# Stick-breaking stages of a head pair two weight units apart, and the S5 input stage of layer 1 one unit later

## The reference, cut to what matters

```python
z = jnp.einsum('bhqd,bhkd->bhqk', qb, k).astype(jnp.float32) * scale
log_1mb = jnp.where(mask, jax.nn.log_sigmoid(-z), 0.0)
later = lax.cumsum(log_1mb, axis=3, reverse=True) - log_1mb
w = jnp.where(mask, jnp.exp(jax.nn.log_sigmoid(z) + later), 0.0)
return jnp.einsum('bhqk,bhkd->bhqd', w.astype(v.dtype), v)
```

## The kernel before, in words

| pause of unit | layer 0 before | layer 1 before | layer 0 and 1 after |
|---|---|---|---|
| 6 | sb_s 0 (and mm_k in layer 0) | sb_s 0 | the same |
| 7 | sb_u 0 | sb_u 0 | none |
| 8 | sb_p 0, sb_s 1 | the same | sb_u 0, sb_s 1 |
| 9 | sb_u 1 | the same | none |
| 10 | sb_p 1, sb_s 2 | the same | sb_p 0, sb_u 1, sb_s 2 |
| 11 | sb_u 2 | the same | none |
| 12 | sb_p 2, sb_s 3 | and ssm_in 0 | sb_p 1, sb_u 2, sb_s 3 |
| 13 | sb_u 3, ssm_in 0 | sb_u 3, ssm_in 1 | ssm_in 0 |
| 14 | sb_p 3, ssm_in 1 | sb_p 3, ssm_in 2, ssm_out 0 | sb_p 2, sb_u 3, ssm_in 1 |
| 15 | ssm_in 2, ssm_out 0, turn | ssm_in 3, ssm_out 1, turn | ssm_in 2, ssm_out 0, turn |
| 16 | da_s 0, ssm_in 3, ssm_out 1 | da_s 0, ssm_out 2 | sb_p 3, da_s 0, ssm_in 3, ssm_out 1 |
| 17 | da_t 0, da_s 1, ssm_out 2 | da_t 0, da_s 1, ssm_out 3 | da_t 0, da_s 1, ssm_out 2 |
| 18 | da_p 0, da_t 1, da_s 2, ssm_out 3 | da_p 0, da_t 1, da_s 2 | with ssm_out 3 |

## Time and profile before

### The profile page before, as it was taken

One profiled execution on the slowest core, in us unless ns is written; L12 is line 12 of the kernel. 1 busy time (PEld: TensorE's weight loads), 2 busy tenths in 40 slices (PEclk: granted clock), 3 DMA queues, 4 the chain that ended last, 5 costly groups with the idle time before them and its releaser, 6 DMA issues. The chain is left out here.

```text
span 1025.0 us, 17644 instructions
## 1 busy us (share of the span) xinstructions
PE 990.7 (97%) x6784; PEld 877.4 (86%) x6784; DVE 765.7 (75%) x1185; ACT 550.5 (54%) x843; POOL 46.2 (5%) x104
## 2 busy tenths in 40 slices
PE   6999999999999999999999999999999999999996
PEld 6977899999897888888889779999988878888885
DVE  5988997888765866889765569787887567666665
ACT  7455436475755645544464663545656565444543
POOL 5004000000000004000000110000000000000000
PEclk9999999999999999999999999999999999999999
DMA  8797438556644666686657853465665446666661
GB/s 330 240 187 181 124 104 268 147 169 182 182 145 123 247 187 185 195 222 190 195 145 203 178 149 100 142 197 149 180 181 167 141 127 188 191 193 189 185 190 78
DMA packets 64163, 181.37 MB, mean 177 GB/s; under 512 B 19728, under 2 KB 21776, under 8 KB 63440
## 3 DMA queue, kind: packets, MB, share of 16 engines
q1 hardware_dynamic: 63648, 179.91, 60.6%
q10 hardware_dynamic: 432, 0.32, 0.1%
HBM read 176.67 MB, written 3.54 MB: 176 GB/s over the span
## 5 line engine op out<-in xcount | busy, mean ns | idle before, releaser
L1288 DVE TENSOR_TENSOR s_w_lo<-s_raw,s_w_hi 128x1024 fp32r<-128x1024 f32 x312 | 374.9, 1228 | 95.4 <-ACT s_w_hi L914 91.6
L914 ACT ACTIVATE s_w_hi<-s_raw 128x1024 fp32r<-128x1024 f32 x312 | 320.8, 1054 | 183.1 <-PE p_T L1876 76.7
L1874 PE MATMUL p_T<-s_hT,s_w_hi 128*128 128x256 f32 x576 | 165.8, 288 | 0.7 <-ACT s_w_hi L914 0.7
L1875 PE MATMUL p_T<-s_hT,s_w_hi 128*128 128x256 f32 x576 | 162.9, 283 | 0.0
L1876 PE MATMUL p_T<-s_hT,s_w_lo 128*128 128x256 f32 x576 | 162.8, 283 | 0.0
L1874 PE MATMUL p_A<-s_w_hi,s_bT_hi 128*128 128x512 f32 x320 | 125.1, 391 | 2.5 <-DVE s_bT_lo L1288 2.5
L1876 PE MATMUL p_A<-s_w_hi,s_bT_lo 128*128 128x512 f32 x320 | 124.7, 390 | 0.0
L1875 PE MATMUL p_A<-s_w_lo,s_bT_hi 128*128 128x512 f32 x320 | 124.6, 389 | 0.0
L1874 PEld LDWEIGHTS p_T<-s_hT,s_w_hi 128*128 128x128 f32 x576 | 110.2, 191 | 4.6 <-issue 2.7
L1875 PEld LDWEIGHTS p_T<-s_hT,s_w_hi 128*128 128x128 f32 x576 | 110.3, 192 | 0.1
L1876 PEld LDWEIGHTS p_T<-s_hT,s_w_lo 128*128 128x128 f32 x576 | 110.3, 192 | 0.0
(11 more groups left out here) (269 smaller groups left out, 1844.1 us busy)
## 6 DMA issues: line engine op xcount, KB each, us to landing
s_raw<-in_weights SPq DMA_DIRECT2D x312, 512.0 KB, 3.7
s_bt<-in_ssm_bt SPq DMA_DIRECT2D x2, 1024.0 KB, 7.3
s_gates<-f_turn SPq DMA_DIRECT2D x16, 128.0 KB, 7.5
s_x<-in_x SPq DMA_DIRECT2D x1, 1024.0 KB, 10.0
s_dv<-in_ssm_bc SPq DMA_DIRECT2D x2, 512.0 KB, 8.6
u_turn<-s_st_y SPq DMA_DIRECT2D x4, 256.0 KB, 4.7
s_uB<-u_turn SPq DMA_DIRECT2D x16, 64.0 KB, 5.1
s_bt<-in_mem SPq DMA_DIRECT2D x1, 1024.0 KB, 7.0
```

The costliest lines, as they stand in the source:

```text
L914: return nc.scalar.activation(o, i, f, **kw)
L1288: return V.tensor_tensor(o, i0, i1, op)
L1874: mm(o, lhi, rhi, start=first, stop=False, **kw)
L1875: mm(o, lhi, rlo, start=False, stop=False, **kw)
```

## The change

The sums stage moves from one unit after the scores to two, the value products from two units after to four. The banks of sb_u are A0 and A1 in place of X0 and X1. The four ssm_in take A2, X0, A1, A1 in place of A0, A1, A0, A1. `FIRST` of layer 1 becomes 13, so all ssm stages and GELU of layer 1 come one unit later, and with them the two places in SyncE's order where the result of the S5 branch is written out and read back (`turn_y`, from chunk positions 45 and 48 to 47 and 50).

```diff
-FIRST = [13, 12]
+FIRST = [13, 13]
...
     for p in range(SB_PAIRS):
         after(6 + 2 * p, "sb_s", p)
-        after(7 + 2 * p, "sb_u", p)
-        after(8 + 2 * p, "sb_p", p)
+        after(8 + 2 * p, "sb_u", p)
+        after(10 + 2 * p, "sb_p", p)
...
-        "mem_row": ["X0"], "sb_s": ["X0", "X1"], "sb_u": ["X0", "X1"], "sb_p": ["A3"], "turn": ["X0", "X1"],
+        "mem_row": ["X0"], "sb_s": ["X0", "X1"], "sb_u": ["A0", "A1"], "sb_p": ["A3"], "turn": ["X0", "X1"],
...
-        [["A0", "A1"][s[1] % 2]] if s[0] == "ssm_in" else
+        [["A2", "X0", "A1", "A1"][s[1]]] if s[0] == "ssm_in" else
...
-                        act.wait_ge(*st.at(*freed(l, "X0", s)))
-                        act.wait_ge(*st.at(*freed(l, "X1", s)))
+                        act.wait_ge(*st.at(*freed(l, "A0", s)))
+                        act.wait_ge(*st.at(*freed(l, "A1", s)))
...
-                        for h, b in enumerate(("X0", "X1")):
+                        for h, b in enumerate(("A0", "A1")):
                             dve.wait_ge(*st.at(*full_at(l, b, s)))
                             tt(z[:, h, :], z[:, h, :], bank[b][:, 0:384], ALU.subtract)\
...
                         pe.wait_ge(*st.at(nl_ready, s[1] + 1))
-                        for h, b in enumerate(("X0", "X1")):
+                        for h, b in enumerate(("A0", "A1")):
                             pe.wait_ge(*st.at(*before(l, b, s)))
```

## The result

| | kernel before | changed kernel |
|---|---|---|
| median of ten executions, us | 1026.97 | 1031.03 |
| lowest to highest | 1026.31 to 1028.42 | 1027.6 to 1031.5 |
| the profiled execution: time, span | 1026.68, 1025.0 | 1027.6, 1025.9 |

The ratio is 1.0029, with a 95% interval of 1.0021 to 1.0037: slower by 3.0 us (2.2 to 3.8). The medians lie 4.1 apart. The forecast was 1027.5 with 1025.6 to 1029.8, so it missed. The executions come apart by the mean clock that the chip granted TensorE. Two are at 0.998 and take 1027.6 and 1028.41, one is at 0.996 with 1029.54, and seven are at 0.994 to 0.995 with 1030.64 to 1031.5. The profile is the fastest of the ten, so by itself it would mislead. An execution without any fall reads 0.997 to 0.998 and not 1.0: the clock also goes down once TensorE has finished, in the kernel before from 1021.3 us to the end of the span at 1025.0.

What follows compares the result with a forecast made beforehand. TensorE, busy 97% of the span at full clock, was taken as the bound; the terms 0 + 0.6 - 1.07 + 1.72 - 0.81 + 0 = +0.44 on 1027.1 gave 1027.5 us, range 1025.6 to 1029.8 (8 in 10).

Steps and rivals of the forecast that it cites:

- R4: Rival, 5%: the wait in pause 13 of layer 0 lets TensorE's clock fall, costing about 2.3 us, to 1029.8.
- (a): Stage contents in TensorE's pauses: the same instructions are moved, not removed, and a stop itself costs almost nothing; 0.
- (b): Changes of matmul tile at the pauses' seams: three more per layer at 0.1 us each, +0.6 us.
- (c): TensorE's waits for `nl_ready` before sb_u, five in both layers, go: -1.07 us.
- (d): Pause 13 of layer 0: ssm_in 0 waits 2.26 us for `bt_ready` in place of 0.54, +1.72 us.
- (e): Pause 17 of layer 0: da_t 0 no longer waits for bank A1, -0.81 us.
- (f): Layer 1, stages one unit later with FIRST = 13: no new TensorE wait, 0, up to +0.8 us.
- S: Start of the last matmul of unit 12 in layer 0, from which the `bt_ready` wait is counted.
- R1: Rival, 12%: each pause itself costs time, so six fewer stops bring a gain; 1025.2 us, the edge of faster.
- R3: Rival, 9%: a late chunk in front of p_bt 2 in layer 0 delays `bt_ready`; slower, 1031.3 us with 4.2 late.

Runs made afterwards that it cites:

- experiment 1: The changed kernel run again with nothing altered: 1031.0 us median, ratio 1.0039.
- experiment 3: The changed kernel with the last p_bt part of layer 0 moved from unit 12 to unit 11, so `bt_ready` comes earlier: 1027.67 us, ratio 1.0007.
- experiment 4: The kernel before with ssm_in 0 put in front of sb_u 3 in pause 13 of layer 0: 1032.35 us, ratio 1.0051.
- experiment 2: The changed kernel with ten extra matmuls in front of the wait for `bt_ready` in pause 13 of layer 0: 1028.38 us median.
- experiment 5: The changed kernel with sb_u 3 of layer 0 kept in pause 13, in front of ssm_in 0: 1026.44 us, ratio 0.9992.

## Why the prediction was wrong, point by point

The rival R4, TensorE's clock, is what happened. It was given 5% and 1029.8. Its place (pause 13 of layer 0) and its mechanism were right. The step that failed is the clock's term: the forecast's sum has it at nothing. The only rows behind that were two waits of 0.85 and 0.93 from start to start, at which the clock had stayed full. They say nothing of one three times as long. The fall came in at least 11 of 15 executions, and the profiled one cost 2.8 us where R4 has 2.3. With it the sum comes out: 1027.0 for the kernel before, 1.1 for the terms below and 2.8 make 1030.9, and 1031.03 was measured. The two executions in which the clock held, 1027.6 and 1028.41, lie by the forecast of 1027.5.

The section of the Trainium skill that was cited with it ("TensorE: Matmul & The Clock Gate", "HAM oscillation — how this bites in real kernels") warns of idle gaps that throttle the engine again. The trace of experiment 1 agrees in kind, with an idle gap of 2.65 us at whose end the clock fell.

By the terms of the sum, from profiles in which the clock held:

| term | forecast | measured |
|---|---|---|
| (a) contents, six stops fewer | 0 | about -0.3 |
| (b) seams | +0.6 | about +1.1 |
| (c) waits for `nl_ready` | -1.07 | about -1.0 |
| (d) wait for `bt_ready` | +1.72 | +2.17 |
| (e) wait of da_t 0 | -0.81 | -0.8 |
| (f) layer 1 stalls | 0 | 0 |
| pause 18 of layer 0, da_t 1 no longer late | not named | -0.1 |
| sum | +0.44 | about +1.1 |
| the clock | 0 | +2.8 where it falls |

The total is read from two starts: unit 19 of layer 0 begins 0.8 later than before, and the mixer stretch of layer 1 adds 0.3; the span is 0.9 longer. The terms are read pause by pause, so they hold to about 0.1.

(c) and (e) came out as forecast. (a) was not quite nothing. From the second matmul of unit 7 to the last of unit 8 the kernel before takes 12.25 us with pause 7 in it, the changed one 10.44 without: 1.81, of which sb_u 0 is 1.74. So a stop costs about 0.06, and six of them are gone. (b) was mis-sized: sb_u between sb_p and sb_s changes the tile on both sides, 0.11 before it and 0.10 behind, not one 0.1. Pause 10 costs 3.78 (81.46 to 85.70, less two steps of 0.23), against 1.86 + 1.74 = 3.60 for its parts, and pauses 12 and 14 and the same three of layer 1 pay about as much. (d) was mis-sized by 0.45: the count let masking start behind the subtractions and forgot that sb_s 3 now stands last in the pause. Masking waits for its scores, and starts at S + 4.1 and not S + 3.65 (96.16 to 100.27). The overlooked order lengthened the very wait on which the clock hung.

R1 was wrong: 0.06 for each stop is too little for it, and the new wait is large. R3 didn't happen: the two preps in front of p_bt 2 begin right behind the work before them (102.42). But its count was tight: p_bt 1 ends at 98.52, and VectorE goes on to sb_p 1 at once (98.56); only the 0.23 of idleness before masking shows slack. That the wait could not be won back by an earlier `bt_ready` (experiment 3) was not foreseen. The first part of the prediction says that VectorE is as close to full there as TensorE, but the argument for (d) did not use it.

Not settled: why the clock holds in two of 15 executions with the same wait, and why the profiled fall is 6.8 us long in experiment 1 and 3.4 in experiment 4. No run here tells.

## What to carry to other kernels

When a stage is moved away from in front of a wait, price the wait twice: its length, and what the clock does behind it. A wait that TensorE spends in two pieces around some matmuls can cost more in clock than in waiting once it is one piece (2.8 us against 2.2 more of waiting here). A single profile may be of an execution that escaped; the mean clock of every execution shows it. Where such a wait can't be avoided, put useful matmuls, or even useless ones, into it.

## What the runs showed of the hardware that was not expected

The clock fell at a wait of 3.03 us without a matmul start (2.65 us idle) in at least 11 of 15 executions; in the one profiled it stood at 1.2 GHz for 6.8 us. It never fell in 22 with ten or five matmuls of 512 columns in that place once the other weak place was filled, though with five 1.51 us of idleness in one piece were left. At the start of layer 1 the idleness is only 1.3 us, among transposes and matmuls of 64 columns, and the clock still fell there for 3.4 us in three profiles (experiments 2, 4 and 5); 21 of 96 executions of the kernel before have the mean clock of such a fall, 0.996. 0.9 us of extra matmuls there ended it in all 44 executions of the four kernels that had them. So a fall is a matter of chance from one execution to the next, and the upper part of the spread of the kernel before, 1027.7 to 1029, is mostly made of them.

A matmul whose tile differs from its forerunner's came 0.09 to 0.11 us later here than its forerunner's columns account for (128x128 to 128x64, 64x64 or 64x128, and back): 0.32 instead of 0.23, 0.32 instead of 0.22, 0.75 instead of 0.64.
